# The value-gate product of a convolution module: from GpSimd to VectorE, read out of PSUM between the taps

## The chip, the core and the metric

The kernel runs on one NeuronCore of a Trainium2 chip. The core has five engines that run side by side and wait for one another by semaphores: TensorE (PE; its weight loads are listed as PEld), VectorE (DVE), ScalarE (ACT), GpSimd (POOL) and SyncE (SP), which here only starts DMAs. Matrix products land in PSUM, which has eight banks of 128 x 512 float32; everything else lies in SBUF. The metric is the device time of one launch in microseconds.

## The reference, cut to what matters

One decoder layer over 2048 prompt tokens and 8 sample tokens of width 1024. Ahead of the experts stands a mixer:

```
z  = h @ w_in                                  # 1024 -> 1536
u  = z[..., :512]; v = z[..., 512:1024]; gt = z[..., 1024:]
d, _ = multi_scale_pool(u, ...)                # trailing means over 2, 4, 8, 16 rows, minus u
a  = v * sigmoid(gt)                           # the value-gate product
yc = causal_depthwise_conv(a, ..., w_dw, b_dw) # 31 taps along the tokens
yn = layer_norm(yc) * ln_g + ln_b
mix = concat([d @ w_pool * pool_scale, silu(yn)]) @ w_out
x  = x + g1 * mix                              # then a norm, the router, 64 experts, a final norm
```

All of it is float32. The change concerns `a = v * sigmoid(gt)` for the prompt tokens alone.

## The kernel before

The program has a front (conditioning vectors, mixer, routing; up to about 1200 us), a stage over blocks of routed tokens (to about 3100 us) and a final norm. Only the front's mixer is touched.

The mixer works in steps of 256 tokens (SUP), two tiles of 128. Step s runs `w_in` and the pooling differences for its own 256 tokens and, at the same time, convolution, layer norm, `w_out`, residual and norm for the 256 tokens of step s-1; in later steps also routing for the step before. Steps 0 to 7 have their own tokens, steps 1 to 8 a convolution, so steps 1 to 7 have both. Channels lie in four chunks (CH) of 128. There is no planner: every engine has its own instruction list written out by hand, and the order on an engine is the order of the code.

- **TensorE** (`step`, L1351): `w_pool` products, then `w_in` in twelve pieces (L1299), each a PSUM bank of 128 x 256 summed over 8 slices: four pieces u, then in turn gate 0, value 0, gate 1, value 1, and so on. The first six (`w_in_mm(0)`) stand before the other six (`w_in_mm(1)`), with a transpose and router logits of the previous step between them. All pieces use two banks in turn, `zb[0]` and `zb[1]`, and a bank may be filled again once it was emptied, which `z_drained` counts. Behind `w_in` stand the transposes of the next input (L1273), of the convolution's result (`y_T`, L1305), of the normed rows (`yn_T`, L1312) and then `w_out` (L1321).
- **ScalarE** empties the banks: u to `u_buf` (L665), the gate through a sigmoid to `sgt` (L671, two buffers), the value as a copy to `vv` (L674, two buffers). A gate's buffer is written again only after `a_ready` has counted the product that read it.
- **GpSimd** (`step`, L514) multiplies `sgt` by `vv` into `av` (`amul`, L501) and computes the pooling differences (`diff`, L484 to L493), in the order amul 0, diff 0, amul 1, diff 1, amul 2, diff 2, amul 3. Then it takes the power -1/2 for the two layer norms (`power`, L473, which waits for `lnv`), then diff 3, then from step 3 on 16 indirect DMAs (`scatter`, L511), and then the two powers for the next norm (waiting for `x1_ms`).
- **VectorE** scales the next input, copies `av` into `a_buf`, and runs `conv` (L887): 4 chunks x 31 taps, the first tap L900, the other 120 instructions L903, each `y = window * weight + y` over 128 x 256. Then norms (`norm`, L907: statistics L910 to L912, L914 after GpSimd's power), routing, residual (L922) and the second norm (L935, after GpSimd's power).

Of the kernel before, what the change touches and what calls it, by code (L numbers as in the profile page):

```python
# [11 lines left out]
ALU = mybir.AluOpType  # L12
# [3 lines left out]
P = 128  # L16
# [3 lines left out]
NS = 8  # L20
# [80 lines left out]
def program(nc, a, const, out):  # L101
# [72 lines left out]
    y = f("y", [P, CH, SUP]); dd = f("dd", [P, CH, SUP]); mixP = f("mixP", [P, CH, SUP]); mixC = f("mixC", [P, TPS, CH, P])  # L174
    sgt = f("sgt", [P, 2, SUP]); vv = f("vv", [P, 2, SUP]); pa = f("pa", [P, 2, POOLB + SUP])
    xin = [f("xin0", [P, D]), f("xin1", [P, D])]; xres = f("xres", [P, D]); x1b = f("x1b", [P, D]); h2 = f("h2", [P, D])
# [267 lines left out]
    def _(pool):  # L444
# [69 lines left out]
        def step(s, has_in, has_next, has_post, has_scatter, first=False):  # L514
            if has_next:
                for j in range(TPS):
                    power(st[:, 2 + j:3 + j], st[:, 4 + j:5 + j], S["xms"], xt.step(), S["xrs"])
            if has_in:
                for j in range(CH):
                    amul(s, j, has_post)  # L520
                    if j < CH - 1:
                        diff(s, j, first, has_post)
            if has_post:
                for j in range(TPS):
                    power(st[:, 6:7], st[:, 7:8], S["lnv"], lt_i.now + j + 1, S["lnr"])
            if has_in:
                diff(s, CH - 1, first, has_post)
            z.step((CH if has_post else 0) + (ZC if has_in else 0) + (TPS if has_post else 0))
# [12 lines left out]
        step(2, True, True, True, False)  # L541
        with rolled(pool, NSUP - 4, {z: CH + ZC + TPS, xt: TPS, lt_i: TPS}) as i:
            step(i + 3, True, True, True, True)
# [75 lines left out]
    def _(act):  # L619
# [222 lines left out]
    def _(dve):  # L842
# [43 lines left out]

        def conv(p, first):  # L887
# [126 lines left out]

        def step(s, has_next, has_post, has_late, kind=""):
            if has_next:
                for j in range(TPS):
                    xn_ms(j)
                for j in range(TPS):
                    xn(j, xt.now - 1 + j)  # L1020
            if has_post:
                conv(s - 1, kind == "second")
            if has_post:
                if kind == "second":
                    bcast(h2)
# [26 lines left out]
        dve.wait_ge(S["pool_const"], 9)  # L1052
        step(0, True, False, False)
        step(1, True, True, False, kind="second")
        step(2, True, True, True)
        with rolled(dve, NSUP - 4, {cv: CH * TAPS, xt: TPS, ti: TPS}) as i:
            step(i + 3, True, True, True)
        step(NSUP - 1, False, True, True)

# [5 lines left out]
        V.tensor_tensor(hT[:, :, 0:NS], xsT[:], B1T[:, :, 0:NS], ALU.add).then_inc(S["sm_h"], 1)  # L1065
        step(NSUP, False, True, True)
        zs = (NSUP - 1) * (CH + TPS) + NSUP * ZC
        dve.wait_ge(S["z_drained"], zs + 1)
# [175 lines left out]
    def _(pe):  # L1244
        M = nc.tensor
        tpu, z, xt, ti, kd = Tally(), Tally(), Tally(), Tally(), Tally()
        pe.wait_ge(S["const_in"], 128)
# [32 lines left out]

        def zbank():

            wait(pe, S["z_drained"], z.now - 1)
            b = zb[z.n % 2]
            z.step()
            return b

        def pool_mm(p, src, nt):
            for g_ in range(CH):
                b = zbank()  # L1290
                M.matmul(b[:, 0:nt], w_pool[:, g_, :], src[:, g_, 0:nt], start=True, stop=True).then_inc(S["zp_filled"], 1)

        def w_in_mm(part):

            order = list(range(CH)) + [c for j in range(CH) for c in (2 * CH + j, CH + j)]
            for m in order[:CH + 2] if part == 0 else order[CH + 2:]:
                b = zbank()
                for k in range(KD):
# [8 lines left out]

        def yn_T(i, nt=P):
            pe.wait_ge(S["ly_drained"], i + 1)
            b = zbank()  # L1310
            for c in range(CH):
# [116 lines left out]
        yn_T(NTILE, NS)  # L1428
        w_out_mm(NTILE, 0, z.now, NS)

        edges = [(u_buf, 0, POOLB), (a_buf, SUP, CONVB), (usm, 0, NS), (asm, 0, NS)]
        for i, (t, c0, n) in enumerate(edges):
            if i < 2:
                wait(pe, S["z_drained"], z.now - 1)
            else:
                pe.wait_ge(S["edge_ready"], i - 1)
            b = zb[z.n % 2]
            z.step()
            for c in range(CH):
                last = M.transpose(b[0:n, c * P:(c + 1) * P], t[:, c, c0:c0 + n], ident[:])  # L1440
# [139 lines left out]
```

## Time and profile before

| | |
|---|---|
| time, median of 3 runs | 3223.34 us (3217.88 to 3224.4) |
| the profiled execution, first to last instruction | 3224.1 us |
| busy PE, DVE, ACT, POOL | 2685.4, 1778.0, 1058.2, 1147.3 us |
| mean granted clock of TensorE | 0.922 of full speed |

The profiled execution has no time of its own besides its span; the span lies within the runs and 0.8 us above their median. Each row of the sections below gives a start, a duration, the engine, the line in the source, the operation, and what is written from what. A bracket at a row's end gives the idle time of the engine before it and what ended it. The times of step 3 (440 to 554 us) stand for those of all seven steps.

### The profile page before, as it was taken

The numbers are of one execution on the slowest core, as the hardware profiler recorded it, in microseconds if no ns is written. First come the engines' busy times: TensorE is split into PE (matmuls) and PEld (weight loads), VectorE is DVE, ScalarE is ACT, GpSimd is POOL, SyncE is SP. The second block draws the span as 40 slices with busy tenths as digits, with TensorE's granted clock in tenths as the row PEclk, the third lists the DMA queues.
The fourth block names the chain that finished last, engine by engine and source line by source line (L and its number), as shares of the span: only waits on it lengthen the run. The fifth ranks groups of instructions, "written<-read, shape, count | busy, mean of one in ns | idle before, by whom it ended". The sixth has DMA issues, their size and how long they took to land.

```text
span 3224.1 us, 56738 instructions
## 1 busy us (share of the span) xinstructions
PE 2685.4 (83%) x11753; PEld 2015.7 (63%) x11754; DVE 1778.0 (55%) x3601; ACT 1058.2 (33%) x2213; POOL 1147.3 (36%) x1173
## 2 busy tenths in 40 slices
PE   6897787778777839999999998989999999999940
PEld 1174564555565517877777777777777777777730
DVE  1034785785677754355554466565645544445558
ACT  1022212112111213244443355454534443344411
POOL 0025525644753342323233322223332232232337
PEclk9998898898887769999999999999999999999975
DMA  7751001001000306567776688888887677667665
GB/s 267 294 228 43 30 33 53 20 33 59 7 33 33 121 16 191 116 193 226 220 214 181 187 253 245 230 254 241 252 225 217 194 211 207 182 177 195 174 177 203
DMA packets 255795, 518.50 MB, mean 161 GB/s; under 512 B 18222, under 2 KB 154375, under 8 KB 255588
## 3 DMA queue, kind: packets, MB, share of 16 engines
q1 hardware_dynamic: 199108, 327.34, 29.4%
q0 software_dynamic: 56624, 190.48, 24.7%
q8 instruction: 21, 0.34, 0.0%
q14 instruction: 42, 0.34, 0.0%
HBM read 386.48 MB, written 131.99 MB: 161 GB/s over the span
## 4 chain that ended last, share of the span: by engine, by line
PE 53%; POOL 15%; DMA 12%; issue 10%; DVE 5%; ACT 3%; ACTq 1%; DVEq 1%; POOLq 1%; SPq 0%
PE zb L1465 22%; PE mx L1465 11%; PE zb L1299 7%; POOL b_av L501 7%; DMA b_xg<-hf_d,b_gidx 5%; PE tp L1478 4%; POOL list_d L511 4%; DMA acc_d<-b_ob,b_sidx 3%; PE mx L1321 3%; PE zb L1263 2%; DMA b_big<-in_w_ada 2%; PE zb L1414 1%; ACT b_wh L794 1%; DVE b_wl L1168 1%; POOL b_pa L484 1%
## 5 line engine op out<-in xcount | busy, mean ns | idle before, releaser
L595 POOL DMA_INDIRECT acc_d<-b_ob,b_sidx x180 | 310.8, 1727 | 1067.2 <-DVE b_ob L1193 556.4
L1465 PE MATMUL zb<-b_wh,b_xh 128*128 x1448 | 589.7, 407 | 53.3 <-issue 33.8
L1465 PE MATMUL zb<-b_wh,b_xl 128*128 x1448 | 572.8, 396 | 0.0
L1465 PE MATMUL zb<-b_wl,b_xh 128*128 x1448 | 572.2, 395 | 0.0
L1168 DVE TENSOR_TENSOR b_wl<-b_win,b_wh (+1 forms) x780 | 481.3, 687 | 132.1 <-ACT b_wh L794 131.8
L794 ACT CAST b_wh<-b_win (+1 forms) x780 | 419.8, 621 | 147.0 <-issue 113.3
L1299 PE MATMUL zb<-b_hT,b_win 128*128 128x256 f32 x1536 | 364.9, 402 | 95.6 <-ACT b_sgt L671 94.6
L1299 PEld LDWEIGHTS zb<-b_hT,b_win 128*128 128x128 f32 x1536 | 310.7, 204 | 149.0 <-ACT b_sgt L671 97.4
L903 DVE SCALAR_TENSOR_TENSOR b_y<-b_a_buf,b_wdw,b_y 128x256 f32<-128x256 f32 x960 | 380.7, 481 | 0.0
L1465 PEld LDWEIGHTS zb<-b_wh,b_xh 128*128 128x128 f32 x1448 | 273.5, 189 | 131.3 <-issue 72.6
L1145 DVE SCALAR_TENSOR_TENSOR b_hh<-b_sgx,b_lt,zb 128x256 f32<-128x256 f32 x181 | 86.9, 480 | 477.7 <-ACT b_sgx L779 476.5
L1465 PE MATMUL mx<-b_wh,b_hth 128*128 x720 | 301.8, 419 | 35.5 <-issue 34.8
L1465 PEld LDWEIGHTS zb<-b_wh,b_xl 128*128 128x128 f32 x1448 | 273.3, 189 | 64.1
L1465 PEld LDWEIGHTS zb<-b_wl,b_xh 128*128 128x128 f32 x1448 | 273.9, 189 | 56.1
L501 POOL TENSOR_TENSOR b_av<-b_sgt,b_vv 128x256 f32<-128x256 f32 x32 | 224.2, 7007 | 182.2 <-ACT b_vv L674 182.2
L1465 PE MATMUL mx<-b_wh,b_htl 128*128 x720 | 287.2, 399 | 0.0
L1465 PE MATMUL mx<-b_wl,b_hth 128*128 x720 | 287.0, 399 | 0.0
L779 ACT ACTIVATE b_sgx<-zb 128x256 f32<-128x256 f32 x181 | 69.4, 383 | 608.7 <-PE zb L1465 608.7
L1193 DVE COPY b_ob<-mx 128x512 f32<-128x512 f32 x180 | 124.2, 690 | 258.6 <-PE mx L1465 165.5
L1152 DVE TENSOR_TENSOR b_xl<-tp,b_xh 128x512 fp32r<-128x512 f32 x364 | 235.0, 686 | 37.6 <-ACT b_xh L785 33.3
L556 POOL DMA_INDIRECT b_xg<-hf_d,b_gidx x183 | 181.2, 990 | 155.3 <-POOL b_gidx L574 144.4
L1478 PE MATMUL tp<-b_ident,b_xg 128*128 128x128 f32 x1456 | 194.2, 277 | 38.6 <-DMA b_xg<-hf_d,b_gidx 38.5
(242 smaller groups left out, 3211.8 us busy)
## 6 DMA issues: line engine op xcount, KB each, us to landing
b_win<-in_w_gate SPq DMA_DIRECT2D x64, 1024.0 KB, 6.3
b_win<-in_w_up SPq DMA_DIRECT2D x64, 1024.0 KB, 12.4
b_win<-in_w_down SPq DMA_DIRECT2D x64, 1024.0 KB, 14.5
b_big<-in_w_ada SPq DMA_DIRECT2D x12, 2048.0 KB, 9.0
acc_d<-b_x1b SPq DMA_DIRECT2D x1, 9216.0 KB, 35.0
b_xin<-in_x_prompt SPq DMA_DIRECT2D x16, 512.0 KB, 3.2
b_big<-in_w_ada_final SPq DMA_DIRECT2D x4, 2048.0 KB, 8.1
b_xres<-in_x_prompt SPq DMA_DIRECT2D x16, 512.0 KB
```

The costliest lines, as they stand in the source:

```text
L501: G.tensor_tensor(av[:, j, :], sgt[:, j % 2, :], vv[:, j % 2, :], ALU.mult).then_inc(S["a_ready"], 1)
L511: G.indirect_dma_start(list_d, bass.IndirectOffsetOnAxis(ap=rows[0:nt, j, k:k + 1], axis=0), pairs[0:nt, j, k, :], None).then_inc(S["scat" ...
L556: G.indirect_dma_start(xg[j][:], None, hf_d, bass.IndirectOffsetOnAxis(ap=gidx[j][:, 0:1], axis=0)).then_inc(S["gath"][j], 16)
L595: G.indirect_dma_start(acc_d, bass.IndirectOffsetOnAxis(ap=sidx[1 - j][:, 0:1], axis=0), ob[1 - j][:], None, compute_op=ALU.add).then_inc( ...
L794: A.copy(wh[:, ds(sn * UW + u, 1), :], stage[:, ds(sn * UW + u, 1), :]).then_inc(S["w_hi"], 1)
L903: ins = V.scalar_tensor_tensor(y[:, c, :], win_, wdw[:, c, k:k + 1], y[:, c, :], ALU.mult, ALU.add)
L1152: V.tensor_tensor(xl[:, k, :], tp[h][:].rearrange("p (k t) -> p k t", k=4), xh[:, k, :].bitcast(F32), ALU.subtract).then_inc(S["gx_lo"], 1)
L1168: V.tensor_tensor(wl[:, at, :], stage[:, at, :], wh[:, at, :].bitcast(F32), ALU.subtract).then_inc(S["w_lo"], 1)
L1193: V.tensor_copy(ob[1 - j][:, 512:1024], mx[1][:]).then_inc(S["o_dve"], 1)
L1299: last = M.matmul(b[:, 0:SUP], win[:, k, m * P:(m + 1) * P], hT[:, k, :], start=(k == 0), stop=(k == KD - 1))
L1465: last = M.matmul(o, lhs, rhs, start=(first and n == 0), stop=(final and n == len(terms) - 1))
L1478: last = M.transpose(tp[h][:, kk * P:(kk + 1) * P], xg[j][:, k * P:(k + 1) * P], ident[:])
```

## The change

The product moves from GpSimd to VectorE and reads the value out of its PSUM bank, so the copy `vv` disappears. VectorE's convolution of step s-1 holds the four products of step s, behind taps 12, 19, 23 and 28. A value bank now counts as emptied when `a_ready` counts its product (`zbank_v`), other banks when `z_drained` counts. The product's arguments are `zb[1]` (the value) and `sgt` (the gate). The other hunks change counts of semaphores only: values no longer count in `z_drained`, so `ZA`, `ZSTEP` and the tally `za` stand in place of `ZC` and `z`, and `behind` says how many banks may be undrained.

```diff
@@ gpsimd @@
-        def amul(s, j, post):
-            zv = z.now + (CH if post else 0) + CH + 2 * j + 1
-            pool.wait_ge(S["z_drained"], zv + 1)
-            if post:
-                pool.wait_ge(S["a_taken"], s)
-            G.tensor_tensor(av[:, j, :], sgt[:, j % 2, :], vv[:, j % 2, :], ALU.mult).then_inc(S["a_ready"], 1)
...
-                for j in range(CH):
-                    amul(s, j, has_post)
-                    if j < CH - 1:
-                        diff(s, j, first, has_post)
+                for j in range(CH - 1):
+                    diff(s, j, first, has_post)
@@ scalar @@
-                act.wait_ge(S["zw_filled"], wn.step())
-                A.copy(vv[:, j % 2, :], zb[z.n % 2][:, 0:SUP]).then_inc(S["z_drained"], 1)
+                wn.step()
@@ vector @@
+        def amul(s, j, first):
+            dve.wait_ge(S["zw_filled"], ZC * s + CH + 2 * j + 2)
+            dve.wait_ge(S["z_drained"], (0 if first else ZSTEP * s - TPS) + CH + j + 1)
+            V.tensor_tensor(av[:, j, :], zb[1][:, 0:SUP], sgt[:, j % 2, :], ALU.mult).then_inc(S["a_ready"], 1)
...
+                if has_in and k in (12, 19, 23, 28):
+                    amul(p + 1, (12, 19, 23, 28).index(k), False)
@@ tensor @@
+        def zbank_v(empties):
+            if empties:
+                pe.wait_ge(S["a_ready"], zv.now)
+            else:
+                wait(pe, S["z_drained"], za.now - 1)
+            b = zb[z.n % 2]
+            z.step()
+            return b
...
-                b = zbank()
+                if m < CH or m == 2 * CH:
+                    b = zbank()
+                elif m >= 2 * CH:
+                    b = zbank(0)
+                else:
+                    b = zbank_v(m > CH)
+                    zv.step()
```

VectorE in step 2, around the convolution, before (a number is the row's place in the engine's list; brackets give the semaphores waited for):

```order
66 L892 COPY b_a_buf<-b_av 128x4x256
67 L900 TENSOR_SCALAR b_y<-b_a_buf,b_wdw,b_vecT 128x256 [waits ly_filled,a_taken]
68 L900 TENSOR_SCALAR b_y<-b_a_buf,b_wdw,b_vecT 128x256 x3
69 L903 SCALAR_TENSOR_TENSOR b_y<-b_a_buf,b_wdw,b_y 128x256 [waits conv_link] x120
70 L910 BN_STATS b_bn<-ly 128x6 [waits ly_filled]
```

The same place after the change (L901 is the old L903, L883 the product):

```order
75 L890 COPY b_a_buf<-b_av 128x4x256
76 L898 TENSOR_SCALAR b_y<-b_a_buf,b_wdw,b_vecT 128x256 [waits ly_filled,a_taken]
77 L898 TENSOR_SCALAR b_y<-b_a_buf,b_wdw,b_vecT 128x256 x3
78 L901 SCALAR_TENSOR_TENSOR b_y<-b_a_buf,b_wdw,b_y 128x256 [waits conv_link] x48
79 L883 TENSOR_TENSOR b_av<-zb,b_sgt 128x256 [waits z_drained,zw_filled]
80 L901 SCALAR_TENSOR_TENSOR b_y<-b_a_buf,b_wdw,b_y 128x256 [waits conv_link] x28
81 L883 TENSOR_TENSOR b_av<-zb,b_sgt 128x256 [waits z_drained,zw_filled]
82 L901 SCALAR_TENSOR_TENSOR b_y<-b_a_buf,b_wdw,b_y 128x256 [waits conv_link] x16
83 L883 TENSOR_TENSOR b_av<-zb,b_sgt 128x256 [waits z_drained,zw_filled]
84 L901 SCALAR_TENSOR_TENSOR b_y<-b_a_buf,b_wdw,b_y 128x256 [waits conv_link] x20
85 L883 TENSOR_TENSOR b_av<-zb,b_sgt 128x256 [waits z_drained,zw_filled]
86 L901 SCALAR_TENSOR_TENSOR b_y<-b_a_buf,b_wdw,b_y 128x256 [waits conv_link] x8
```

The 120 instructions are cut at 48, 76, 92 and 112, and a product stands in each cut. On TensorE the second half of `w_in` in step 2 keeps its order (gate 1, value 1, gate 2, value 2, gate 3, value 3) and its waits become these; L1321 is the old L1299:

```order
155 L1321 MATMUL zb<-b_hT,b_win 128x256 [waits z_drained]
156 L1321 MATMUL zb<-b_hT,b_win 128x256 x7
157 L1321 MATMUL zb<-b_hT,b_win 128x256 [waits a_ready]
158 L1321 MATMUL zb<-b_hT,b_win 128x256 x7
159 L1321 MATMUL zb<-b_hT,b_win 128x256 [waits z_drained]
160 L1321 MATMUL zb<-b_hT,b_win 128x256 x7
161 L1321 MATMUL zb<-b_hT,b_win 128x256 [waits a_ready]
162 L1321 MATMUL zb<-b_hT,b_win 128x256 x7
```

Before, each of these waited for `z_drained`; now each value piece waits for the product before it on VectorE.

## Rows read from the trace of the kernel before

**Rows 1.** The page: chain shares by line, two costly groups (count, busy, mean, idle).

```profile
PE zb L1465 22%; PE mx L1465 11%; PE zb L1299 7%; POOL b_av L501 7%; DMA b_xg<-hf_d,b_gidx 5%; PE tp L1478 4%; POOL list_d L511 4%; DMA acc_d<-b_ob,b_sidx 3%; PE mx L1321 3%; PE zb L1263 2%; DMA b_big<-in_w_ada 2%; PE zb L1414 1%; ACT b_wh L794 1%; DVE b_wl L1168 1%; POOL b_pa L484 1%
...
L903 DVE SCALAR_TENSOR_TENSOR b_y<-b_a_buf,b_wdw,b_y 128x256 f32<-128x256 f32 x960 | 380.7, 481 | 0.0
...
L501 POOL TENSOR_TENSOR b_av<-b_sgt,b_vv 128x256 f32<-128x256 f32 x32 | 224.2, 7007 | 182.2 <-ACT b_vv L674 182.2
```

**Rows 2.** Line L501 by itself: count, duration min/median/max in ns.

```profile
L501 POOL TENSOR_TENSOR b_av<-b_sgt,b_vv x32: 717/725/31006, 183.7 to 968.5; 128x256 f32<-128x256 f32 x32
```

**Rows 3.** Timeline of DVE in step 3: start, duration, instruction, idle before.

```profile
443.66 47.59 DVE L903 SCALAR_TENSOR_TENSOR b_y<-b_a_buf,b_wdw,b_y 128x256 f32<-128x256 f32 x120
503.70 0.70 DVE L910 BATCH_NORM_STATS2 b_bn<-ly 128x6 f32<-128x512 f32 x1 [12.46 <-PE ly L1305]
...
505.67 0.81 DVE L914 TENSOR_SCALAR b_yn<-ly,b_bn,b_st 128x512 f32<-128x512 f32 x1 [0.68 <-POOL b_st L473]
...
537.72 1.28 DVE L935 SCALAR_TENSOR_TENSOR b_h<-b_x1b,b_st,b_A2b 128x1024 f32<-128x1024 f32 x1 [6.38 <-POOL b_st L473]
```

**Rows 4.** Timeline of POOL in step 3.

```profile
463.62 28.21 POOL L501 TENSOR_TENSOR b_av<-b_sgt,b_vv 128x256 f32<-128x256 f32 x1 [23.12 <-ACT b_vv L674]
491.79 0.63 POOL L484 TENSOR_TENSOR b_pa<-b_u_buf 128x270 f32<-128x270 f32 x1
492.60 0.86 POOL L487 TENSOR_SCALAR b_pa<-b_pa 128x256 f32<-128x256 f32 x1 [0.17 <-POOL b_pa L484]
493.66 0.73 POOL L492 TENSOR_TENSOR b_dd<-b_pa,b_u_buf 128x256 f32<-128x256 f32 x1 [0.20 <-POOL b_pa L487]
...
494.72 0.72 POOL L501 TENSOR_TENSOR b_av<-b_sgt,b_vv 128x256 f32<-128x256 f32 x1
495.40 0.64 POOL L484 TENSOR_TENSOR b_pa<-b_u_buf 128x270 f32<-128x270 f32 x1
...
498.98 0.73 POOL L501 TENSOR_TENSOR b_av<-b_sgt,b_vv 128x256 f32<-128x256 f32 x1
499.66 0.63 POOL L484 TENSOR_TENSOR b_pa<-b_u_buf 128x270 f32<-128x270 f32 x1
...
504.02 0.73 POOL L501 TENSOR_TENSOR b_av<-b_sgt,b_vv 128x256 f32<-128x256 f32 x1
505.06 0.57 POOL L473 TENSOR_TENSOR b_st<-b_st,b_half 128x1 f32<-128x1 f32 x1 [0.31 <-DVE b_st L912]
...
537.00 0.58 POOL L473 TENSOR_TENSOR b_st<-b_st,b_half 128x1 f32<-128x1 f32 x1
```

**Rows 5.** Timeline of PE in step 3.

```profile
440.14 22.62 PE L1299 MATMUL zb<-b_hT,b_win 128*128 128x256 f32 x96
...
466.35 14.03 PE L1299 MATMUL zb<-b_hT,b_win 128*128 128x256 f32 x64
492.30 10.06 PE L1299 MATMUL zb<-b_hT,b_win 128*128 128x256 f32 x32 [11.91 <-ACT b_sgt L671]
...
503.06 0.60 PE L1305 MATMUL ly<-b_ident,b_y 128*128 128x128 f32 x4
```

**Rows 6.** Waits of DVE from 200 to 1010 us: total, times, longest.

```profile
DVE b_bn L910 <- PE ly L1305: 93.4, 14, 12.5
...
DVE b_h L935 <- POOL b_st L473: 41.5, 13, 8.9
```

**Rows 7.** Line L1156, DVE, one PSUM and one SBUF input: min/median/max ns.

```profile
L1156 DVE TENSOR_TENSOR b_htl<-ly,b_hth x181: 412/418/427, 1231.9 to 3100.1; 128x256 fp32r<-128x256 f32 x181
```

**Rows 8.** Timelines: POOL's first power and PE's `w_out`, steps 2 and 7.

```profile
392.55 0.57 POOL L473 TENSOR_TENSOR b_st<-b_st,b_half 128x1 f32<-128x1 f32 x1 [0.34 <-DVE b_st L912]
...
398.87 5.40 PE L1321 MATMUL mx<-b_big,b_mixP 128*128 128x512 f32 x8 [3.76 <-ACT b_mixC L681]
...
969.15 0.57 POOL L473 TENSOR_TENSOR b_st<-b_st,b_half 128x1 f32<-128x1 f32 x1
...
972.87 5.26 PE L1321 MATMUL mx<-b_big,b_mixP 128*128 128x512 f32 x8 [1.16 <-ACT b_mixC L681]
```

More of the change, by code:

```diff
@@ L31 @@
 KE = DE // P
+ZA = 2 * CH
+ZSTEP = CH + ZA + 2
 SCALE = 2.5
@@ L174, in program @@
     y = f("y", [P, CH, SUP]); dd = f("dd", [P, CH, SUP]); mixP = f("mixP", [P, CH, SUP]); mixC = f("mixC", [P, TPS, CH, P])
-    sgt = f("sgt", [P, 2, SUP]); vv = f("vv", [P, 2, SUP]); pa = f("pa", [P, 2, POOLB + SUP])
+    sgt = f("sgt", [P, 2, SUP]); pa = f("pa", [P, 2, POOLB + SUP])
     xin = [f("xin0", [P, D]), f("xin1", [P, D])]; xres = f("xres", [P, D]); x1b = f("x1b", [P, D]); h2 = f("h2", [P, D])
@@ L527, in step @@
                 diff(s, CH - 1, first, has_post)
-            z.step((CH if has_post else 0) + (ZC if has_in else 0) + (TPS if has_post else 0))
+            z.step((CH if has_post else 0) + (ZA if has_in else 0) + (TPS if has_post else 0))
             if has_scatter:
@@ L541, in _ @@
         step(2, True, True, True, False)
-        with rolled(pool, NSUP - 4, {z: CH + ZC + TPS, xt: TPS, lt_i: TPS}) as i:
+        with rolled(pool, NSUP - 4, {z: ZSTEP, xt: TPS, lt_i: TPS}) as i:
             step(i + 3, True, True, True, True)
@@ L885, in xn, with conv @@
             V.tensor_scalar(xin[j][0:nt, :], xin[j][0:nt, :], st[0:nt, 4 + j:5 + j], None, ALU.mult).then_inc(S["xn_ready"], 1)
-        def conv(p, first):
+        def amul(s, j, first):
+            dve.wait_ge(S["zw_filled"], ZC * s + CH + 2 * j + 2)
+            dve.wait_ge(S["z_drained"], (0 if first else ZSTEP * s - TPS) + CH + j + 1)
+            V.tensor_tensor(av[:, j, :], zb[1][:, 0:SUP], sgt[:, j % 2, :], ALU.mult).then_inc(S["a_ready"], 1)
+        def conv(p, first, has_in=False):
             dve.wait_ge(S["a_ready"], CH * p + CH)
@@ L1013, in lists_free, with step @@
                 wait(dve, q, 16 * TOPK * group)
-        def step(s, has_next, has_post, has_late, kind=""):
+        def step(s, has_in, has_next, has_post, has_late, kind=""):
             if has_next:
@@ L1021, in step @@
             if has_post:
-                conv(s - 1, kind == "second")
+                conv(s - 1, kind == "second", has_in)
+            else:
+                for j in range(CH):
+                    amul(s, j, True)
             if has_post:
@@ L1052, in _ @@
         dve.wait_ge(S["pool_const"], 9)
-        step(0, True, False, False)
-        step(1, True, True, False, kind="second")
-        step(2, True, True, True)
+        step(0, True, True, False, False)
+        step(1, True, True, True, False, kind="second")
+        step(2, True, True, True, True)
         with rolled(dve, NSUP - 4, {cv: CH * TAPS, xt: TPS, ti: TPS}) as i:
-            step(i + 3, True, True, True)
-        step(NSUP - 1, False, True, True)
+            step(i + 3, True, True, True, True)
+        step(NSUP - 1, True, False, True, True)
         xn_ms(0, NS)
@@ L1065, in _ @@
         V.tensor_tensor(hT[:, :, 0:NS], xsT[:], B1T[:, :, 0:NS], ALU.add).then_inc(S["sm_h"], 1)
-        step(NSUP, False, True, True)
-        zs = (NSUP - 1) * (CH + TPS) + NSUP * ZC
+        step(NSUP, False, False, True, True)
+        zs = ZSTEP * NSUP - CH - TPS
         dve.wait_ge(S["z_drained"], zs + 1)
@@ L1245, in _ @@
         M = nc.tensor
-        tpu, z, xt, ti, kd = Tally(), Tally(), Tally(), Tally(), Tally()
+        tpu, z, za, zv, xt, ti, kd = Tally(), Tally(), Tally(), Tally(), Tally(), Tally(), Tally()
         pe.wait_ge(S["const_in"], 128)
@@ L1279, in xT_, with zbank @@
             rows_T(src, nt, S["xt_filled"])
-        def zbank():
-            wait(pe, S["z_drained"], z.now - 1)
+        def zbank(behind=1):
+            wait(pe, S["z_drained"], za.now - behind)
+            b = zb[z.n % 2]
+            z.step()
+            za.step()
+            return b
[4 more added lines that the diff above has]
+                wait(pe, S["z_drained"], za.now - 1)
             b = zb[z.n % 2]
@@ L1286, in zbank, with pool_mm @@
             return b
-        def pool_mm(p, src, nt):
+        def pool_mm(p, src, nt, behind_v=False):
             for g_ in range(CH):
-                b = zbank()
+                if behind_v and g_ == 1:
+                    pe.wait_ge(S["a_ready"], zv.now)
+                b = zbank(0 if behind_v and g_ == 0 else 1)
                 M.matmul(b[:, 0:nt], w_pool[:, g_, :], src[:, g_, 0:nt], start=True, stop=True).then_inc(S["zp_filled"], 1)
@@ L1296, in w_in_mm @@
             for m in order[:CH + 2] if part == 0 else order[CH + 2:]:
-                b = zbank()
+                if m < CH or m == 2 * CH:
+                    b = zbank()
+                elif m >= 2 * CH:
+                    b = zbank(0)
+                else:
+                    b = zbank_v(m > CH)
+                    zv.step()
                 for k in range(KD):
@@ L1306, in y_T, with yn_T @@
             last.then_inc(S["ly_filled"], 1)
-        def yn_T(i, nt=P):
+        def yn_T(i, nt=P, behind=1, behind_v=False):
             pe.wait_ge(S["ly_drained"], i + 1)
-            b = zbank()
+            if behind_v:
+                pe.wait_ge(S["a_ready"], zv.now)
+            b = zbank(behind)
             for c in range(CH):
@@ L1354, in step @@
                 pe.wait_ge(S["d_ready"], CH * s)
-                pool_mm(s - 1, dd, SUP)
+                pool_mm(s - 1, dd, SUP, not has_late)
             if has_in:
@@ L1371, in step @@
             if has_post:
-                yn_T(i)
-                z0 = z.now
+                yn_T(i, behind=0 if has_in else 1)
+                z0 = za.now
                 y_T(i + 1, y, P)
                 w_out_mm(i, 0, z0)
-                yn_T(i + 1)
+                yn_T(i + 1, behind_v=has_in)
                 if has_late:
                     ranks(i)
-                w_out_mm(i + 1, 1, z.now)
+                w_out_mm(i + 1, 1, za.now)
                 h_T(i)
@@ L1404, in _ @@
         step(2, True, True, True, True)
-        with rolled(pe, NSUP - 4, {tpu: 2 * TPS, z: CH + ZC + TPS, xt: TPS, ti: TPS, kd: 1}) as i:
+        with rolled(pe, NSUP - 4, {tpu: 2 * TPS, z: CH + ZC + TPS, za: ZSTEP, zv: CH, xt: TPS, ti: TPS, kd: 1}) as i:
             step(i + 3, True, True, True, True)
@@ L1428, in _ @@
         yn_T(NTILE, NS)
-        w_out_mm(NTILE, 0, z.now, NS)
+        w_out_mm(NTILE, 0, za.now, NS)
         edges = [(u_buf, 0, POOLB), (a_buf, SUP, CONVB), (usm, 0, NS), (asm, 0, NS)]
@@ L1433, in _ @@
             if i < 2:
-                wait(pe, S["z_drained"], z.now - 1)
+                wait(pe, S["z_drained"], za.now - 1)
             else:
@@ L1438, in _ @@
             z.step()
+            za.step()
             for c in range(CH):
```

## Prediction

> **What bounds the kernel now.** I read the chain by line first: L501, the product on GpSimd, holds 7% of the span, with a mean of 7007 ns over 32 [rows 1]. The naive reading is a slow instruction worth 224 us. The line by itself says otherwise: its median is 725 ns and its longest 31.0 us [rows 2]. With 25 instructions at 0.72 us (18 us), the other 206 us belong to seven, 29.4 us each: one per step 1 to 7. The timelines say why. In step 3 VectorE's 120 taps run without a gap from 443.66 to 491.25; GpSimd's product starts at 463.62 and ends at 491.83, 0.6 us behind the last tap; the next three need 0.72 us each [rows 3, 4]. GpSimd is held off while the taps run, so the 28 us are the convolution's time written on another engine. The convolution stays. What the product costs is what it makes late.
>
> That is read behind the last tap (call its end C). TensorE did `w_in` pieces up to 480.4 and then stood until ScalarE could reuse `sgt`, which waits for that product; its last two pieces run at 492.30 to 502.4, behind C, and `y_T`, which needs nothing but the convolution, queues behind them until 503.06 [rows 5]. VectorE idles 12.46 us [rows 3]. Over the steps that wait is 93.4 us in 14 times; the short ones, one per step, are near 1.3 us, which leaves 12.0 us per step [rows 6]. Behind it GpSimd's first layer-norm power starts at 505.06, that is 1.36 us behind VectorE's L910 [rows 3, 4]; with 0.2 us for three steps in which GpSimd came later still, C to this power (call it T) is 13.6 us per step. GpSimd itself reaches T only 0.3 us before it is asked: amul 3 ends near 504.75 [rows 4]. Two paths tie there; shortening one alone brings little.
>
> Behind T all hangs on T. In steps 3 to 7 GpSimd's diff 3, 16 scatters and the power at 537.00 follow in order, and VectorE waits for that power (6.38 us in step 3; 41.5 us in 13 waits) [rows 3, 4, 6].
>
> **The change part by part.**
>
> TensorE: in step 3 the first six pieces end at 462.76 and a product behind tap 12 stands at 443.66 + 48 x 0.397 = 462.7 (47.59 us over 120 taps is 0.397 each). Piece value 1 ends about 473.4, tap 19 about 11.1 us behind the first product; values 2 and 3 at 480.4 and, at 3.5 us a piece, 487.4, against taps 23 and 28 at about 481.5 and 490.5 [rows 3, 5]. So the products find their banks filled within some tenths of a us, and all twelve pieces fit under the taps. `y_T` can start at C instead of C + 11.8, and L912 be done at about C + 2.2. This removes the one path wholly.
>
> ScalarE: 32 copies go; it waits elsewhere, so I count nothing.
>
> VectorE: four products per step, now on the path that sets C. The nearest row is a 128 x 256 product with one PSUM and one SBUF input at 418 ns [rows 7]; taps of 481 ns follow one another each 397 ns, so I take 0.34 us, plus 0.1 us for two semaphores: 1.7 us per step. Bounds: 0.3 (hidden waits) and 0.9 us each.
>
> GpSimd: it loses the products, but not the differences, and those are held off by the taps just as the product was. The first add of diff 0 now starts when u 0 is in SBUF, about 446, inside the taps. If it gets no chance until the end, it ends at about C + 0.54, as the product did (491.79), and what is left is 495.40 - 492.60 less one product (0.68), so 2.12, then diff 1 (495.40 to 498.98, 3.58) and diff 2 (499.66 to 504.02, 4.36) [rows 4]: with a 0.17 gap T is C + 10.8. This is the wait that takes the place of the removed one: TensorE's and VectorE's work is ready at C + 2.2, GpSimd's queue is not.
>
> The products may open a door: a tap reads two SBUF operands, the product one. If GpSimd gets in beside each, its four instructions of diff 0 (0.63, 0.86, 0.73 and the small copy) run during the taps, the next tap waits for what is left of them beyond the 0.34 us (0.3, 0.5, 0.4, 0: 1.2 us), and behind C remain the pending first add (0.54 + 0.17), 2.8 of diff 1 (3.58 less its first add and a gap, 0.8) and 4.36 of diff 2: T at C + 7.9, with C later by 1.7 + 1.2 = 2.9, say 3.0. No row here shows a product beside taps. I take this value, since the taps' held-off engine asks for the port all the time, and keep the other end.
>
> A rule of the Trainium skill bears on it. The trace first: the wait is 28 us, over some 70 taps of 0.48 us [rows 1, 4]. The page "SBUF — State Buffer", section "Who interferes with whom", says that a VectorE instruction with two SBUF inputs contends with a GpSimd instruction that reads SBUF, the later one blocking for the whole instruction, and that one with a single SBUF input does not contend. By the first half alone GpSimd would lose one tap, not seventy; here the measurement goes further than the page. By the second half the door opens; without it, it stays shut.
>
> The sum: per step 13.6 - 7.9 - 3.0 = 2.7 us, times 7 = 18.9. In steps 1 and 2, without scatters, `w_out` is next: it starts 6.3 us behind T in step 2, since ScalarE still drains the next input and loads its table, but 3.7 us in step 7, where it has no such work [rows 8]. With those drains done earlier the steps 1 and 2 gain 2.6 us each, 5 in all; in steps 3 to 7 the scatters hide it. Nothing else moves: the experts' stage starts earlier by the same amount. 18.9 + 5 = 24, less 1 for step 1, whose first product waits about 1 us for its bank: 23 us. The profile's span is 3224.1 us, 0.8 us above the runs' median, so 3224.1 - 23 = 3201 us.
>
> **The rivals.**
>
> The door stays shut: per step 13.6 - 10.8 - 1.7 = 1.1, times 7 = 7.7, plus 5, less 1: 12 us, 3212. For it: seventy taps let nothing through. Against: the product needs one SBUF operand less.
>
> GpSimd stops being late: its differences fit wholly under the taps at no price, and T is C + 2.2. Then 13.6 - 2.2 - 1.7 = 9.7 per step, 68 + 5 = 73 us: 3151. For it speaks the gap of 12 us that everybody sees; against it that a difference can only run when taps do not.
>
> GpSimd, once in, keeps the port for its whole chain: diff 0 to 2 (2.93 + 3.58 + 4.36 = 10.9 us) go into the convolution, T is C + 2.2: 13.6 - 2.2 - 1.7 - 10.9 = -1.2 per step, -8 + 5: 3227, which cannot be told from no change. Against it: GpSimd leaves gaps of 0.17 us between its instructions [rows 4], and a waiting tap should take them.
>
> Slower: the products wait for their banks. VectorE runs in order, so all taps behind a product wait, and C with them. At the rate of the last two pieces (10.06 us for 32 products, against 14.03 for 64) [rows 5] six pieces would take 30 us, not 21, and value 3 would come 6 us late; that GpSimd would use for its differences, so it would still cost nothing much. It decides from about 9 us per step. With pieces at twice 3.5 us value 3 comes at 508.4, 18 us behind its tap: 13.6 - 2.2 - 1.7 - 18 = -8.3 per step, -58 + 5: 3277. Against it: the pieces at 466 ran at full rate while the taps ran.
>
> **How the numbers follow.** A measurement here can tell about 0.2%, 6.4 us, from no change. The forecast, door open, has 0.57 (3190 to 3208, as a product costs 0.3 to 0.9 us and GpSimd gets in three to five times); door shut 0.22 (3206 to 3219); GpSimd no longer late 0.08; GpSimd keeps the port 0.08; banks late 0.05. The range 3186 to 3217 holds the first case and nearly all of the second. Faster by over 0.2% (below 3217): 0.57 + 0.19 + 0.08 = 0.84; within: 0.03 + 0.08 = 0.11; slower: 0.05.
>
> **What would show it.** Right: TensorE's twelve pieces end before the last tap; VectorE's L910 waits 1 us, not 12; in its place L914 waits some 6 us for GpSimd's power; the first add of diff 0 is long, and diff 0 is done before the last tap; the taps span 50 to 51 us. Door shut: that add lasts to C, and L914 waits near 9 us. Wrong: taps with gaps of several us, or a power at C + 2.

## The result and the profile after

The kernel after takes 3185.57 us (median of 4 runs, 3177.5 to 3188.59) against 3222.7 us before (4 runs): ratio 0.9883, 95% interval 0.9868 to 0.9898. That is 37 us less where 23 us were forecast, 0.4 us below the range's lower end. The profiled run took 3186.78 us, with a span of 3185.0 us.

The gain lies where the prediction put it. The convolution of step 1 starts at 215.71 us (216.91 before), that of step 8 at 983.45 (1022.11): of 38.7 us, 37.5 are won in steps 1 to 7, between 4.2 and 6.4 in each.

VectorE in step 3, timeline (start, duration, operation, count; the bracket is idle time ahead and what ended it):

```profile
430.03 1.38 DVE L898 TENSOR_SCALAR b_y<-b_a_buf,b_wdw,b_vecT 128x256 f32<-128x256 f32 x4
431.33 19.08 DVE L901 SCALAR_TENSOR_TENSOR b_y<-b_a_buf,b_wdw,b_y 128x256 f32<-128x256 f32 x48
450.64 0.42 DVE L883 TENSOR_TENSOR b_av<-zb,b_sgt 128x256 f32<-128x256 f32 x1 [0.23 <-PE zb L1321]
450.98 14.83 DVE L901 SCALAR_TENSOR_TENSOR b_y<-b_a_buf,b_wdw,b_y 128x256 f32<-128x256 f32 x28
465.74 0.41 DVE L883 TENSOR_TENSOR b_av<-zb,b_sgt 128x256 f32<-128x256 f32 x1
...
481.00 3.24 DVE L901 SCALAR_TENSOR_TENSOR b_y<-b_a_buf,b_wdw,b_y 128x256 f32<-128x256 f32 x8
485.44 0.70 DVE L910 BATCH_NORM_STATS2 b_bn<-ly 128x6 f32<-128x512 f32 x1 [1.21 <-PE ly L1327]
487.41 0.81 DVE L914 TENSOR_SCALAR b_yn<-ly,b_bn,b_st 128x512 f32<-128x512 f32 x1 [0.69 <-POOL b_st L476]
490.35 0.70 DVE L910 BATCH_NORM_STATS2 b_bn<-ly 128x6 f32<-128x512 f32 x1 [2.13 <-PE ly L1327]
520.03 1.28 DVE L935 SCALAR_TENSOR_TENSOR b_h<-b_x1b,b_st,b_A2b 128x1024 f32<-128x1024 f32 x1 [7.65 <-POOL b_st L476]
```

The last tap ends (C) at 484.24. The wait of 12.46 us in [rows 3] is 1.21 us now, and L914 does not wait for GpSimd's queue (0.69 us). But the 28 taps behind the first product take 14.83 us where 28 undisturbed ones take 28 x 0.397 = 11.1: 3.7 us more.

GpSimd in the same step:

```profile
433.82 17.09 POOL L487 TENSOR_TENSOR b_pa<-b_u_buf 128x270 f32<-128x270 f32 x1 [5.65 <-ACT b_u_buf L658]
451.09 1.08 POOL L490 TENSOR_SCALAR b_pa<-b_pa 128x256 f32<-128x256 f32 x1 [0.17 <-POOL b_pa L487]
452.38 1.00 POOL L495 TENSOR_TENSOR b_dd<-b_pa,b_u_buf 128x256 f32<-128x256 f32 x1 [0.20 <-POOL b_pa L490]
453.53 0.20 POOL L496 COPY b_u_buf<-b_u_buf 128x15 f32<-128x15 f32 x1 [0.15 <-POOL b_dd L495]
453.68 0.88 POOL L487 TENSOR_TENSOR b_pa<-b_u_buf 128x270 f32<-128x270 f32 x1
...
462.51 0.20 POOL L496 COPY b_u_buf<-b_u_buf 128x15 f32<-128x15 f32 x1
486.80 0.57 POOL L476 TENSOR_TENSOR b_st<-b_st,b_half 128x1 f32<-128x1 f32 x1 [24.09 <-DVE b_st L912]
491.71 0.55 POOL L476 TENSOR_TENSOR b_st<-b_st,b_half 128x1 f32<-128x1 f32 x1 [4.34 <-DVE b_st L912]
```

The first add of diff 0 is held off for 17 us and ends at 450.91, while the first product runs. Then not one instruction follows but all: by 462.71, some 12 us later and 21.5 us ahead of C, GpSimd is done with diffs 0, 1 and 2, and waits 24 us until it is asked. The first layer-norm power (T) stands at 486.80, C + 2.56; before it was C + 13.81 [rows 3, 4].

In this kernel it is VectorE's wait for the product's bank, and not the product, that lets the add in. In steps 1, 2, 3 and 7 the add ends 0.50 us behind the last tap ahead of the product, whenever the product comes; an add takes 0.63 us undisturbed, so it had begun before. In step 1 it ends 1.9 us before the product starts:

```profile
232.85 3.25 DVE L901 SCALAR_TENSOR_TENSOR b_y<-b_a_buf,b_wdw,b_y 128x256 f32<-128x256 f32 x8
238.51 0.42 DVE L883 TENSOR_TENSOR b_av<-zb,b_sgt 128x256 f32<-128x256 f32 x1 [2.41 <-PE zb L1321]
221.69 14.90 POOL L487 TENSOR_TENSOR b_pa<-b_u_buf 128x270 f32<-128x270 f32 x1 [7.40 <-ACT b_u_buf L658]
```

That a product without a wait lets GpSimd in as well is seen in two kernels below (the product from SBUF, and diff 1 late). In steps 4, 5 and 6 no door is needed: the add arrives 0.15 to 0.27 us behind the first L901 tap, takes 0.70 to 0.82 us, and nothing is held off. Step 4:

```profile
543.27 0.82 POOL L487 TENSOR_TENSOR b_pa<-b_u_buf 128x270 f32<-128x270 f32 x1 [3.31 <-ACT b_u_buf L658]
```

Of the 70 first adds in the ten kernels here that have the product on VectorE, the 28 that came before the first such tap, or up to 0.32 us behind its start, took under 0.9 us; the 42 that came 0.35 us or more behind it were held for 14.9 us or more.

TensorE in step 3:

```profile
466.20 10.63 PE L1321 MATMUL zb<-b_hT,b_win 128*128 128x256 f32 x48 [1.52 <-DVE b_av L883]
484.29 1.12 PE L1327 MATMUL ly<-b_ident,b_y 128*128 128x128 f32 x4 [6.58 <-DVE b_y L901]
489.25 1.06 PE L1327 MATMUL ly<-b_ident,b_y 128*128 128x128 f32 x4
```

All pieces of `w_in` end 7.4 us ahead of C, and `y_T` starts 0.05 us behind it. It takes 1.12 us, against 0.60 in [rows 5]: TensorE had just stood still for 6.58 us.

VectorE's waits between 200 and 1010 us (total us, times, longest):

```profile
DVE b_h L935 <- POOL b_st L476: 43.4, 14, 7.7
DVE b_bn L910 <- PE ly L1327: 21.3, 14, 2.1
DVE b_av L883 <- PE zb L1321: 9.8, 5, 6.5
DVE b_yn L914 <- POOL b_st L476: 9.5, 14, 0.7
```

L910 waits 21.3 us where it waited 93.4; L935's wait is about as long as before (41.5) [rows 6]. Of the products' 9.8 us, 6.5 are in step 0, which has no convolution, and 2.4 in step 1.

### The profile page after: what moved, and what is told of

Read it like the earlier page. It is cut to its first block, busy times and chain, and to the rows that moved or that the text cites. A ratio compares the mean times of both kernels' runs of the same rounds, so it can differ in the third digit from the quotient of the medians.

```text
span 3185.0 us, 56695 instructions
## 1 busy us (share of the span) xinstructions
PE 2697.6 (85%) x11753; PEld 2024.3 (64%) x11754; DVE 1808.1 (57%) x3633; ACT 1048.4 (33%) x2181; POOL 994.4 (31%) x1141
## 4 chain that ended last, share of the span: by engine, by line
PE 57%; issue 14%; POOL 8%; DMA 8%; DVE 7%; ACT 3%; ACTq 1%; DVEq 1%; POOLq 1%; SPq 0%
PE zb L1490 26%; PE mx L1490 13%; PE zb L1321 4%; PE tp L1503 4%; DMA b_xg<-hf_d,b_gidx 4%; POOL list_d L506 4%; PE mx L1345 3%; DVE b_y L901 3%; PE zb L1266 2%; DMA acc_d<-b_ob,b_sidx 2%; DMA b_big<-in_w_ada 1%; POOL b_pa L487 1%; PE zb L1438 1%; PE ly L1534 1%; DVE b_wl L1171 1%
## 5 line engine op out<-in xcount | busy, mean ns | idle before, releaser
L901 DVE SCALAR_TENSOR_TENSOR b_y<-b_a_buf,b_wdw,b_y 128x256 f32<-128x256 f32 x960 | 409.6, 500 | 0.0
L1321 PE MATMUL zb<-b_hT,b_win 128*128 128x256 f32 x1536 | 356.2, 395 | 22.3 <-DVE b_av L883 21.5
L1321 PEld LDWEIGHTS zb<-b_hT,b_win 128*128 128x128 f32 x1536 | 304.2, 199 | 73.5 <-DVE b_av L883 24.3
L476 POOL TENSOR_TENSOR b_st<-b_st,b_half 128x1 f32<-128x1 f32 (+1 forms) x51 | 30.9, 610 | 694.9 <-DVE b_st L912 319.7
```

Source lines behind the costliest of these rows:

```text
L1321: last = M.matmul(b[:, 0:SUP], win[:, k, m * P:(m + 1) * P], hT[:, k, :], start=(k == 0), stop=(k == KD - 1))
```

## The experiments

**What lets GpSimd in: the product on VectorE, or any break in the taps?** The kernel before, its product left on GpSimd, with a one-column fill of a scratch tile:

```diff
+                if k in (14, 20, 24, 28):
+                    V.memset(door[:], 0.0)
```

> The kernel before with one addition: VectorE writes a zero to a 128 x 1 scratch (no SBUF input, no wait) behind taps 14, 20, 24 and 28; the product stays on GpSimd. Theory D (a door): any VectorE instruction without two SBUF inputs lets GpSimd's held-off instruction in, and from then GpSimd and the taps alternate. Then the first product of a step starts near tap 12 and ends at the first door, under 4 us long instead of 28, differences 0 to 2 end before the last tap, TensorE's last two w_in pieces run under the taps, VectorE's wait ahead of L910 falls from 12 us to under 3 us, and the time falls by 20 to 40 us, near that of the changed kernel. Rival M (the move itself): what helped is that the product left GpSimd's queue; doors alone do nothing: the product lasts to the last tap, L910 waits 12 us, the time is within 5 us of before, or up to 4 us longer for the 32 writes.

Measured: 3186.28 us, ratio 0.988 (0.9861 to 0.99). Four fills of 0.06 us, and nothing moved, do what the whole change does. GpSimd in step 3 (L501 is the product; fills at 454.03, 465.04, 475.36 and 482.17):

```profile
450.66 4.01 POOL L501 TENSOR_TENSOR b_av<-b_sgt,b_vv 128x256 f32<-128x256 f32 x1 [21.98 <-ACT b_vv L674]
454.63 0.82 POOL L484 TENSOR_TENSOR b_pa<-b_u_buf 128x270 f32<-128x270 f32 x1
...
461.00 4.67 POOL L501 TENSOR_TENSOR b_av<-b_sgt,b_vv 128x256 f32<-128x256 f32 x1 [2.98 <-ACT b_vv L674]
...
487.97 0.57 POOL L473 TENSOR_TENSOR b_st<-b_st,b_half 128x1 f32<-128x1 f32 x1 [11.57 <-DVE b_st L914]
```

The first product is held until the fill at 454.03, and five instructions get through (the product and diff 0). GpSimd then idles 2.98 us, and the next product is held until the fill at 465.04; from there everything runs. T is C + 2.6 here too.

**Is it the product's one SBUF input?** The product on VectorE, but from ScalarE's SBUF copy, behind taps 14, 20, 24 and 29:

```diff
+            V.tensor_tensor(av[:, j, :], vv[:, j % 2, :], sgt[:, j % 2, :], ALU.mult).then_inc(S["a_ready"], 1)
```

> The product on VectorE between the taps (behind 14, 20, 24, 29), but from ScalarE's copy vv in SBUF, so it has two SBUF inputs like a tap; waits and counts as in the kernel before. Theory D by operands: no door, so the first add of difference 0 lasts until the last tap in the steps where it arrives among the taps, the power is late (VectorE's L914 waits 7 to 9 us), and the time is 5 to 15 us below before. Rival P (a pause): it is the wait on a semaphore, or any instruction that is not a tap, that lets GpSimd in; then the add ends at the first product, and the time is 30 to 40 us below before, as in the changed kernel.

Measured: 3183.93 us, ratio 0.988 (0.9863 to 0.9897). GpSimd and VectorE, step 3:

```profile
432.43 20.63 POOL L484 TENSOR_TENSOR b_pa<-b_u_buf 128x270 f32<-128x270 f32 x1 [5.61 <-ACT b_u_buf L655]
453.23 0.85 POOL L487 TENSOR_SCALAR b_pa<-b_pa 128x256 f32<-128x256 f32 x1 [0.17 <-POOL b_pa L484]
```
```profile
452.14 0.42 DVE L880 TENSOR_TENSOR b_av<-b_vv,b_sgt 128x256 f32<-128x256 f32 x1
452.48 13.66 DVE L898 SCALAR_TENSOR_TENSOR b_y<-b_a_buf,b_wdw,b_y 128x256 f32<-128x256 f32 x24
```

The product starts without a wait, the add ends 0.5 us behind this product that reads two SBUF operands, and all the rest follows. The count of SBUF inputs is not what opens the door, and reading PSUM is worth nothing here.

**The price of the differences, and whether a read of one column is held off.** Diffs 0 to 2 of steps 1 to 7 become an add of one column (and the small copy), so outputs and routing differ and only the front compares.

```diff
+                chain(G.tensor_tensor(pa[:, 0, 0:1], u_buf[:, g_, 0:1], u_buf[:, g_, 1:2], ALU.add))
```

> The changed kernel without the work of differences 0 to 2 in steps 1 to 7 (each is replaced by an add over one column; dd is left as step 0 wrote it, so outputs differ). It measures what GpSimd's work under the taps costs the taps. If 12 us of GpSimd beside the taps cost them 3.7 us per step (28 taps took 14.83 us, others 11.16), the taps span 4 us less per step and the time is 24 to 30 us below the changed kernel, some 3158 us. Rival: the longer taps come from something else (TensorE's or ScalarE's traffic) and stay: time within 6 us of the changed kernel.

Measured: 3142.45 us, 0.975 (0.9733 to 0.9766). From step 1's convolution to step 8's it takes 738.6 us, where the kernel after takes 767.7: 29 us or 4.2 us a step, within the 24 to 30 expected. The first expert product stands 34 us earlier (1143.4 against 1177.8); 4.4 us of that lie ahead of step 1, where nothing was changed, and the remaining 9 us of the median lie where the routing differs. GpSimd and VectorE in step 3:

```profile
421.00 16.62 POOL L484 TENSOR_TENSOR b_pa<-b_u_buf 128x1 f32<-128x1 f32 x1 [5.68 <-ACT b_u_buf L662]
```
```profile
438.16 11.17 DVE L905 SCALAR_TENSOR_TENSOR b_y<-b_a_buf,b_wdw,b_y 128x256 f32<-128x256 f32 x28
```

28 taps without differences take 11.17 us: the differences cost the taps 3.7 us a step. An add of one column waits as long as one of 270 columns.

**Does it stay in once it is in?** Diff 1 is made to wait for the second gate, so that GpSimd pauses behind diff 0:

```diff
+            if post and g_ == 1:
+                pool.wait_ge(S["z_drained"], z.now + CH + CH + 2)
```

> The changed kernel, but difference 1 also waits until ScalarE has emptied gate 1, which comes in the middle of a row of taps, a few us ahead of the second product. If GpSimd gets in only at a door, its first add lasts until that product (3 to 9 us) although difference 0 was in shortly before. If GpSimd, once in, has the taps alternate with it for the rest of the convolution, the add takes 0.6 to 1.0 us.

Measured: 3178.05 us (one run). GpSimd, step 3:

```profile
450.77 0.20 POOL L498 COPY b_u_buf<-b_u_buf 128x15 f32<-128x15 f32 x1 [0.15 <-POOL b_dd L497]
455.83 5.06 POOL L489 TENSOR_TENSOR b_pa<-b_u_buf 128x270 f32<-128x270 f32 x1 [4.87 <-ACT b_sgt L666]
```

After 4.87 us of idle time it is held off again, until the second product at 460.32, which does not wait. While its instructions follow at 0.16 us, it stays in. How long a pause may be shows in the kernel with the fills: seven of its products came amid the taps after 1.14 to 2.06 us of idle time and took 0.75 to 1.04 us; those that came after 2.98, 3.31 and 3.55 us were held for 4.1 to 4.7 us. One of the seven:

```profile
797.79 1.00 POOL L501 TENSOR_TENSOR b_av<-b_sgt,b_vv 128x256 f32<-128x256 f32 x1 [1.90 <-ACT b_vv L674]
```

In the kernel without differences, adds that came after 2.78 to 2.83 us were held as well, for 15.4 to 16.2 us.

**A door of the taps' own kind**, and then one of the product's operation, both on one column, in the kernel before:

```diff
+                    V.scalar_tensor_tensor(door[:], wdw[:, 0, 0:1], vecT[:, 0:1], wdw[:, 0, 1:2], ALU.mult, ALU.add)
...
+                    V.tensor_tensor(door[:], wdw[:, 0, 0:1], vecT[:, 0:1], ALU.mult)
```

> The kernel before with a door of the taps' own kind behind taps 14, 20, 24 and 28: a scalar_tensor_tensor of 128x1 with both inputs in SBUF, its product left on GpSimd. The memset door and the product of two SBUF inputs each let GpSimd in. If any short or unlinked instruction between the taps does (it need not wait for the tap ahead, or its last access is early), GpSimd's L501 starts behind tap 14 and ends within 5 us, and the time is 3183 to 3190 as with the memset. If a change of operation is what opens it, L501 lasts to the end of the convolution (28 us) and the time is 3222 to 3226.

> The kernel before with a tensor_tensor of 128x1 and two SBUF inputs behind taps 14, 20, 24 and 28, in the places where a scalar_tensor_tensor of 128x1 let one GpSimd instruction in each. If the operation makes the difference, a door of this kind lets GpSimd's whole run of instructions in, as the memset and the product of two SBUF inputs did: 3183 to 3190, all differences done before the last tap. If its length or its having two SBUF inputs does, one instruction a door: 3208 to 3215.

Measured: 3211.36 and 3207.9 us (one run each, 11 and 18 us below the kernel before beside them). GpSimd and VectorE with the first:

```profile
455.95 2.79 POOL L501 TENSOR_TENSOR b_av<-b_sgt,b_vv 128x256 f32<-128x256 f32 x1 [23.21 <-ACT b_vv L674]
458.70 10.05 POOL L484 TENSOR_TENSOR b_pa<-b_u_buf 128x270 f32<-128x270 f32 x1
468.92 6.90 POOL L487 TENSOR_SCALAR b_pa<-b_pa 128x256 f32<-128x256 f32 x1 [0.17 <-POOL b_pa L484]
476.02 6.28 POOL L492 TENSOR_TENSOR b_dd<-b_pa,b_u_buf 128x256 f32<-128x256 f32 x1 [0.20 <-POOL b_pa L487]
```
```profile
458.07 0.68 DVE L907 SCALAR_TENSOR_TENSOR b_door<-b_wdw,b_vecT 128x1 f32<-128x1 f32 x1
496.09 0.81 DVE L916 TENSOR_SCALAR b_yn<-ly,b_bn,b_st 128x512 f32<-128x512 f32 x1 [8.12 <-POOL b_st L473]
```

Exactly one instruction per door, in both (with the second door L484 takes 10.05 us, L487 6.89, L492 6.28). This is the forecast's picture, made by another door: T is 495.49, C + 10.0, and L914's counterpart waits 8.1 us. Neither expectation had the doors right: the first had only all or nothing; the second's first branch fell, and its other branch names two causes that this run cannot part.

**Can the scatter go under the convolution too?** In the kernel after, the 16 scatter instructions move ahead of the first power:

```diff
+            if has_scatter:
+                scatter(s - 3)
             if has_post:
                 for j in range(TPS):
                     power(st[:, 6:7], st[:, 7:8], S["lnv"], lt_i.now + j + 1, S["lnr"])
```

> The kernel after, with GpSimd's 16 scatter instructions (20.8 us a step in steps 3 to 7, behind the second layer-norm power before) moved ahead of the first layer-norm power, so that they follow the differences while VectorE's taps run. In the kernel after VectorE's L935 waits 7.65 us per step for the power that stands behind the scatter, and GpSimd is idle from 462.7 to 486.2. Theory A (once in, GpSimd stays in while its instructions follow one another): the scatter, which reads little of SBUF, runs from about 463 to 484, the wait falls from 7.65 to about 1 us, taps pay 1 to 4 us; 3 to 6 us a step in five steps, 15 to 30 us: 3156 to 3171. Theory B (a pause or another kind of instruction shuts the door): the scatter is held off until the convolution ends and the first layer-norm power stands behind it, up to 20 us later: VectorE waits some 10 to 20 us behind the last tap, the step is 5 to 12 us longer, 3210 to 3245.

Measured: 3216.4 us (12 runs, 3199.77 to 3224.52), ratio 0.998 (0.9968 to 0.9991): 31 us lost. GpSimd in step 3:

```profile
459.31 1.19 POOL L506 DMA_INDIRECT list_d<-b_pairs,b_rows  x1 [0.30 <-issue]
460.81 5.64 POOL L506 DMA_INDIRECT list_d<-b_pairs,b_rows  x1 [0.30 <-issue]
466.75 7.95 POOL L506 DMA_INDIRECT list_d<-b_pairs,b_rows  x1 [0.30 <-issue]
490.84 0.59 POOL L476 TENSOR_TENSOR b_st<-b_st,b_half 128x1 f32<-128x1 f32 x1
```

Three get in, three are held, until the products at 465.54 and 473.79 and until C (477.37), and ten are left. T is C + 13.5: L914 waits 11.62 us, and that L935 waits 0.78 instead of 7.65 does not pay for it. This is theory B, though GpSimd's instructions here follow at 0.30 us; what sets a scatter instruction apart from an add was not tried. In step 8, whose convolution holds no product, one of them is held for 46.0 us.

**What the cold TensorE costs.** Extra products ahead of `y_T`, in the kernel after:

```diff
+            if has_in and has_post:
+                wait(pe, S["mix_drained"], i)
+                for k in range(24):
+                    M.matmul(mx[0][:, 0:SUP], win[:, 0, 0:P], win[:, 1, 0:SUP], start=True, stop=True)
```

> The kernel after, with 24 extra 128x256 products on TensorE (of data at hand, written to a bank that is not read) ahead of the convolution's transposes, where TensorE stands idle for 6.6 us and its granted clock falls: the transposes y_T then take 1.12 us against 0.60 before. Theory A (the idle time costs the clock, and the lower clock is on the path): first power to second power back from 4.9 to 4.0 us, y_T to 0.6: 1 to 1.5 us a step, 7 to 10 us in all: about 3176. Theory B (the clock does not move the path; w_out and the experts are warm again by themselves): within 3 us of the kernel after, 3183 to 3189. If the extra work itself delays y_T, 1 to 3 us a step longer: 3195 to 3205.

> Both edits (scatter early, 24 extra products). If both theories A hold the gains add: 3146 to 3164. If the scatter is held off, the extra products change nothing that hangs on it: within 5 us of the scatter alone.

Measured: 3207.5 us, 0.9954 (0.9939 to 0.997); with the scatter early 3226.47 us, 1.0016 (1.0005 to 1.0026). 24 products took 10.53 us, and `y_T` started 3.7 us behind C, as the last branch of the expectation had it (its 3195 to 3205 us were a little low). With the scatter early they cost 10 us more, not within 5 of it: `y_T` is late there too, ahead of the same power. But the two L910 stand at 495.56 and 499.59, 4.03 us apart, where they are 4.91 apart in the kernel after. So with 12:

> The kernel after with the 12 extra products alone. Theory A (the clock that TensorE loses while it waits for the convolution is on the path): y_T 1.12 to 0.60 us and first to second L910 4.91 to 4.03: 1.4 us a step, 10 us in all, 3176 (3172 to 3181). Theory B (no gain, since something else is as late): 3183 to 3189.

Measured: 3176.3 us, 0.9851 (0.9834 to 0.9867). TensorE's granted clock (the figure behind POOL's count) in two stretches of step 3, up to C and on to the second `y_T`, in the kernel after and then with 12 products:

```profile
477.00:484.30 7.30, 0.72 (x8) 0.48 (x6) 7.23 (x19) 2.91 (x8) 0.00 (x0) 0.88 0.20 72
484.30:490.00 5.70, 4.46 (x20) 3.98 (x20) 1.84 (x4) 3.69 (x9) 0.57 (x1) 0.50 0.29 97
```
```profile
471.00:478.30 7.30, 5.91 (x31) 4.94 (x29) 7.25 (x19) 2.90 (x8) 0.00 (x0) 1.00 0.22 72
478.30:483.00 4.70, 2.62 (x20) 2.15 (x20) 1.84 (x4) 3.54 (x9) 0.57 (x1) 1.00 0.42 139
```

Idle for 6.58 us ahead of `y_T`, TensorE transposes at 0.50 (1.2 GHz); kept busy until 1.40 us ahead of it, at 1.00 (2.4 GHz). This is theory A, with 9 us of the 10 expected; the steps hold 6.7 of them (761.0 against 767.7 us from step 1's convolution to step 8's).

**Diff 3 under the convolution**, behind diff 2, and with the 12 products as well:

```diff
-                for j in range(CH - 1):
+                for j in range(CH):
                     diff(s, j, first, has_post)
...
-            if has_in:
-                diff(s, CH - 1, first, has_post)
```

> The kernel after, with diff 3 (GpSimd, 5.7 us a step between the second layer-norm power and the scatter) moved up behind diff 2, so that it follows the other differences without a pause among the taps. Theory A (what follows at 0.16 us stays in): its seven instructions run under the convolution, which pays 1 to 2 us for them; in steps 3 to 7 scatter and the power behind it come 5.7 us earlier and L935's wait falls from 7.65 to about 2; 4 us in five steps, less 1.5 us in each of steps 1 and 2: 17 us, 3168 (3160 to 3176). Theory B (diff 3 is held off until the convolution ends): the first layer-norm power comes about 5 us later, nothing is gained: 3183 to 3200.

> Diff 3 moved up and 12 extra products on TensorE ahead of y_T. 24 of them took 10.5 us and ended 3 us behind the last tap, so that y_T came 3.1 us late, but the time from the first L910 to the second fell from 4.91 to 4.03 us. 12 take 5.3 us and should end 1 us ahead of the last tap. If both hold: 17 + 8 us below the kernel after, 3160 (3150 to 3170).

Measured: 3175.02 us, 0.9848 (0.9832 to 0.9865), and 3175.04 us, 0.9842 (0.9826 to 0.9859): 10 us below the kernel after (whose interval they just clear) and level with the 12 products alone; of the kernels here that leave nothing out these three are the fastest. Together the two edits give no more than either by itself, and lie outside the expected 3150 to 3170. Of the 10 us with diff 3 early the steps hold 5.1 (762.6 against 767.7); 4.3 lie ahead of step 1, where the edit changes nothing and whose start varies from 211.3 to 217.1 us over the runs here. VectorE with diff 3 early, step 3:

```profile
451.39 17.04 DVE L899 SCALAR_TENSOR_TENSOR b_y<-b_a_buf,b_wdw,b_y 128x256 f32<-128x256 f32 x28
```

Diff 3 got in (it ends at 468.50) at 2.2 us more for the taps, and L935's wait falls from 43.4 to 16.2 us in the front. But VectorE's waits for `w_out` and for ScalarE's norm grew by 5 us each (39.2 to 44.6, 19.9 to 24.9): behind L935's wait other work is nearly as late, and the steps won 5 us, not 17.

## Why the prediction was wrong

- **TensorE**: right. The pieces fit under the taps, products wait tenths of a us (step 1's first 2.4 us, where 1 was forecast), `y_T` starts at C. Missed: behind the 6.58 us without work TensorE's granted clock is 0.50 (1.2 GHz), which costs 0.9 us between the two powers in six of the seven steps (4.91 in step 3; 4.04 in step 6, where the clock is back at 1.00 for the second transposes). The run with 12 extra products shows that it is the clock: it won 6.7 us in the steps.
- **VectorE's products**: right, 0.34 us each (step 3: 465.74 to 466.07).
- **GpSimd behind the product**: the step that failed. The prediction had one instruction in per product, so that behind C the pending first add, 2.8 us of diff 1 and 4.36 us of diff 2 were left and T was "at C + 7.9", with C later by 3.0. In the runs everything came in at the first break of the taps: T at C + 2.56 (the prediction's own sign of being wrong, "a power at C + 2"), C later by 5.3 (54.21 less 48.89 us from the convolution's start; 1.6 for products and their waits, 3.7 for contention). In step 3 T comes 11.25 us nearer to C, C is 5.32 later, and the second power 0.87 later behind the first: 5.1 us won, where 2.7 was forecast, and 5.6 with what shifts behind it; over seven steps 37.5, where 23 were forecast.
- **One step for all seven**: the prediction let the first add start some 3.6 us behind the convolution's start, as in step 3 (3.8). In steps 4, 5 and 6 it comes 1.5 us behind it and needs no door. These steps win as much as the others (4.2, 4.9 and 6.4 us).
- **The price**: the rival in which GpSimd keeps the port charged the taps its whole 10.9 us. They paid 3.7, while GpSimd worked through 11.6 us. That "a difference can only run when taps do not" was false: side by side, both run, a little slower. Of the rival in which GpSimd stops being late the T was right (C + 2.2 against C + 2.56), and its price of nothing was not.
- **Why the door opens**: the reason given, one SBUF input, fell with the product from two; in the kernel after, VectorE's wait opened it. The Trainium skill, "SBUF — State Buffer", section "Who interferes with whom", has the later one of two contenders block for the whole instruction. The waits here were 15 to 31 us, over 38 to 78 taps of 0.4 us, so the rows go further than the page.
- **Steps 1 and 2**: the extra 2.6 us each do not stand out (5.0 and 6.1 us won, the others 4.2 to 6.4).

What stays open is why some doors let in a whole run (a fill of one column, a product of 128 x 256 from PSUM or from SBUF) and others a single instruction (128x1 with two SBUF inputs, whichever operation). Neither operation, nor size, nor SBUF inputs parts the two groups alone. In the second group the door itself waits (0.34 to 0.69 us for one column), in the first a tap behind it; whether that is the cause was not tried. Who starts first does not part them either: behind the first one-column door a tap starts 0.02 us ahead of GpSimd's next instruction and GpSimd is held, but in step 3 of the kernel after a tap starts 0.10 us ahead of it too (450.98 against 451.09), and GpSimd gets in.

## What to carry to other kernels

When one engine's short instruction shows tens of microseconds beside an unbroken stream on another, ask first whether it is held off, and try to break the stream with one cheap instruction before moving work: here four fills of 0.06 us gave the whole gain. Let the held-off engine's work be ready in one piece, since a pause of 3 us shut it out again (one of 2 us did not), and early, since what arrived as the stream began was not held. Price it by a run rather than by one rule: whether all, one or no instruction came in depended on the break. Look at every step of a loop before one stands for all. An engine freed from lateness may go idle right ahead of the path; TensorE came back at a granted clock of 0.50 instead of 1.00.

## What the hardware showed that was not expected

- Some 38 to 78 back-to-back `scalar_tensor_tensor` instructions held off a GpSimd instruction for 15 to 31 us, even a 128x1 add (15.2 to 16.6 us); one that arrived as the taps started was not held off (0.82 us in step 4).
- A pause of VectorE of 0.2 us between two of them let GpSimd in, and so did a fill of 0.06 us.
- Inside, 14 GpSimd instructions over 11.6 us cost 28 taps 3.7 us. After up to 2.06 us of idle time the next product still got in at once; after 2.78 us or more adds and products were held off again. Behind the one-column doors with two SBUF inputs, 0.17 us was enough.
- GpSimd's indirect DMA instructions were held off too: 5.64 and 7.95 us against 0.96, and 46.0 us where nothing broke the taps.
